# Fox attention on one core: one PSUM bank for the projections, two for the turned probabilities

## What is computed

```
q = rms_norm(q.reshape(B, S, FOX_HEADS, FOX_DH), q_norm_g)
k = rms_norm(k.reshape(B, S, FOX_HEADS, FOX_DH), k_norm_g)
...
logits = jnp.einsum('bhts,bshd...') + cb[..., None] - c_t[:, :, None, :]
probs = jax.nn.softmax(logits, axis=-1)
return jnp.einsum('bhts,bshd->bthd', probs, vf)
...
o = o * jax.nn.silu(z)
```

## Time and profile before

| | us |
|---|---|
| median of 3 runs (lowest, highest) | 2000.39 (1998.85, 2004.83) |
| the profiled execution | 1997.79 |
| its span, first to last instruction | 1995.9 |
| PE busy | 1876.2 (94% of the span) |
| PEld, DVE, ACT, POOL busy | 1453.8, 938.5, 773.4, 238.8 |

### The profile page before, as it was taken

One profiled execution on the slowest core, in us unless ns is written; L12 is line 12 of the kernel. 1 busy time (PEld: TensorE's weight loads), 2 busy tenths in 40 slices (PEclk: granted clock), 3 DMA queues, 4 the chain that ended last, 5 costly groups with the idle time before them and its releaser, 6 DMA issues. The chain is left out here.

```text
span 1995.9 us, 27109 instructions
## 1 busy us (share of the span) xinstructions
PE 1876.2 (94%) x10220; PEld 1453.8 (73%) x10220; DVE 938.5 (47%) x1723; ACT 773.4 (39%) x1271; POOL 238.8 (12%) x182
## 2 busy tenths in 40 slices
PE   7999999999999998898989999999999999889898
PEld 5888888879797876776878787655555555468687
DVE  3757565665757562755341210243434434466533
ACT  3526253534436261414222221454454544441321
POOL 1212021211212010020000000110111101002000
PEclk9999999999999999998999999999999999989899
DMA  5211010201011100403112110201111110041211
GB/s 129 51 36 32 22 33 22 36 19 43 14 41 33 32 1 1 159 32 127 40 47 85 43 44 14 58 27 41 30 37 38 28 29 20 23 138 53 92 53 45
DMA packets 113793, 92.22 MB, mean 46 GB/s; under 512 B 19776, under 2 KB 95744, under 8 KB 113664
## 3 DMA queue, kind: packets, MB, share of 16 engines
q1 hardware_dynamic: 113664, 90.49, 16.0%
HBM read 81.99 MB, written 8.49 MB: 45 GB/s over the span
## 5 line engine op out<-in xcount | busy, mean ns | idle before, releaser
L404 PE MATMUL gdn_unit<-part_hi,gdn_w_hi 128*128 128x512 f32 x512 | 234.0, 457 | 0.0
L406 PE MATMUL gdn_unit<-part_hi,gdn_w_lo 128*128 128x512 f32 x512 | 202.1, 395 | 0.0
L405 PE MATMUL gdn_unit<-part_lo,gdn_w_hi 128*128 128x512 f32 x512 | 200.7, 392 | 0.0
L1906 DVE CUSTOM_DVE_ANT_0 fa_probs<-fa_scores,fa_decay 128x896 f32<-128x896 f32 (+7 forms) x128 | 97.0, 758 | 126.0 <-PE fa_scores L1721 80.6
L1740 PEld LDWEIGHTS fa_turned<-ident,fa_probs 128*128 128x128 f32 x576 | 61.0, 140 | 105.0 <-issue 52.5
L1740 PE MATMUL fa_turned<-ident,fa_probs 128*128 128x128 f32 x576 | 102.9, 288 | 33.3 <-ACT fa_probs_t L1855 16.0
L1855 ACT ACTIVATE fa_probs_t<-fa_turned 128x512 f32<-128x512 f32 (+1 forms) x96 | 52.2, 544 | 182.3 <-PE fa_turned L1740 181.4
L753 DVE SCALAR_TENSOR_TENSOR x<-gdn_raw,gdn_taps,x 128x512 f32<-128x512 f32 x144 | 119.8, 832 | 5.1
L371 POOL TENSOR_TENSOR gdn_w_lo<-ring,gdn_w_hi 128x1024 fp32r<-128x1024 f32 x31 | 75.1, 2421 | 354.9 <-ACT gdn_w_hi L570 354.9
L1673 PE MATMUL fa_unit<-part_hi,fa_w_hi 128*128 128x512 f32 x256 | 115.0, 449 | 1.5 <-DVE fa_w_lo L1933 1.5
L406 PEld LDWEIGHTS gdn_unit<-part_hi,gdn_w_lo 128*128 128x128 f32 x512 | 96.2, 188 | 21.5
(11 more groups left out here) (279 smaller groups left out, 3986.7 us busy)
## 6 DMA issues: line engine op xcount, KB each, us to landing
ring<-in_gdn_w_in_dram SPq DMA_DIRECT2D x32, 512.0 KB, 4.2
ring<-in_ple_w_gate_dram SPq DMA_DIRECT2D x32, 256.0 KB, 3.0
ring<-in_fox_w_in_dram SPq DMA_DIRECT2D x32, 256.0 KB, 3.3
ring<-in_fox_w_in_dram SPq DMA_DIRECT2D x16, 512.0 KB, 4.8
fa_decay<-c_rows_scratch SPq DMA_DIRECT2D x64, 128.0 KB, 3.0
in_x_tile<-in_x_dram SPq DMA_DIRECT2D x8, 512.0 KB, 6.0
gdn_g_bc<-g_rows_scratch SPq DMA_DIRECT2D x8, 512.0 KB, 8.9
m_old<-in_x_dram SPq DMA_DIRECT2D x8, 512.0 KB, 3.5
```

The costliest lines, as they stand in the source:

```text
L404: pe.matmul(out, w_hi[:, j % 2, k, :], xh[:, k, ts], start=(k == 0), stop=False)
L405: pe.matmul(out, w_hi[:, j % 2, k, :], xl[:, k, ts], start=False, stop=False)
L406: mm = pe.matmul(out, w_lo[:, j % 2, k, :], xh[:, k, ts], start=False, stop=(k == KT - 1))
```

## The change

`unit` becomes one bank in place of two, and `turned` becomes two banks, one for the pieces that ScalarE copies and one for those that VectorE copies. A unit's first matmul now waits until the unit just before it was taken, not the one before that. A turn now waits for the last copy of its own engine, so there is a whole piece in between. `spread` uses the first of the two banks. The number of banks is the same, and so is every engine's order of instructions; the waits and the addresses alone differ.

```diff
-        unit = [ps(f"unit{n}", [P, HALF]) for n in range(2)]
+        unit = ps("unit", [P, HALF])
...
-        turned, result = ps("turned", [P, HALF]), ps("result", [P, HALF])
+        turned, result = [ps(f"turned{n}", [P, HALF]) for n in range(2)], ps("result", [P, HALF])
...
                 if k == 0:
                     pe.wait_ge(w_low, j + 1)
-                    if n >= 2:
-                        pe.wait_ge(unit_taken, n - 1)
-                out, ts = unit[n % 2][:], slice(half * HALF, (half + 1) * HALF)
+                    if n:
+                        pe.wait_ge(unit_taken, n)
+                out, ts = unit[:], slice(half * HALF, (half + 1) * HALF)
...
-                if by:
-                    pe.wait_ge(flip_a, before + 1)
-                elif before:
-                    pe.wait_ge(flip_d, before)
+                if before:
+                    pe.wait_ge((flip_a, flip_d)[by], before)
                 if e in (0, 5) and side == by == 0 and 2 * p + e // 5:
...
                     pe.wait_ge(spread_used, 2 * p + e // 5)
                 for b, j in enumerate(keys(e, quarter)):
-                    mm = pe.transpose(turned[:, b * P:(b + 1) * P], probs[:, n % 3, j * P:(j + 1) * P], c["ident"][:])
+                    mm = pe.transpose(turned[by][:, b * P:(b + 1) * P], probs[:, n % 3, j * P:(j + 1) * P], c["ident"][:])
...
             def spread(p, part):
                 pe.wait_ge(shared, 2 * p + part + 1)
 
-                pe.wait_ge(flip_d, sides_before(p, (5, NT)[part]))
+                pe.wait_ge(flip_a, sides_before(p, (5, NT)[part]))
```

More of the change, by code:

```diff
@@ L1598, in turned_to @@
             return (probs_t[:, head, ks[0]:ks[-1] + 1, at:at + P],
-                    turned[:, 0:len(ks) * P].rearrange("p (j t) -> p j t", t=P))
+                    turned[by][:, 0:len(ks) * P].rearrange("p (j t) -> p j t", t=P))
         @block.sync
@@ L1693, in keep_warm @@
                 for n in range(rounds):
-                    pe.matmul(unit[n % 2][:], w_hi[:, 0, 0, :], xh[:, 0, 0:HALF], start=True, stop=True)
+                    pe.matmul(unit[:], w_hi[:, 0, 0, :], xh[:, 0, 0:HALF], start=True, stop=True)
             def sum_squares(p, kind):
@@ L1759, in spread @@
                 pe.wait_ge(shared, 2 * p + part + 1)
-                pe.wait_ge(flip_d, sides_before(p, (5, NT)[part]))
+                pe.wait_ge(flip_a, sides_before(p, (5, NT)[part]))
                 for e in range(4):
                     at = row(e) % 4 * P
-                    mm = pe.transpose(turned[:, at:at + P], wide[:, e * P:(e + 1) * P], c["ident"][:])
+                    mm = pe.transpose(turned[0][:, at:at + P], wide[:, e * P:(e + 1) * P], c["ident"][:])
                 mm.then_inc(spread_out, 1)
@@ L1821, in take_unit @@
                 act.wait_ge(unit_made, n + 1)
-                step(act.activation(qk[:, it % 2, u // 2, u % 2 * HALF:(u % 2 + 1) * HALF], unit[n % 2][:], ACT.Copy),
+                step(act.activation(qk[:, it % 2, u // 2, u % 2 * HALF:(u % 2 + 1) * HALF], unit[:], ACT.Copy),
                      unit_taken)
@@ L1927, in gate @@
                 dve.wait_ge(spread_out, 2 * p + part + 1)
-                step(dve.tensor_tensor(z, turned[:], z, ALU.mult), spread_used)
+                step(dve.tensor_tensor(z, turned[0][:], z, ALU.mult), spread_used)
                 dve.wait_ge(weighed, 4 * p + 2 * part + 2)
```

## The result

The changed kernel takes 1968.26 us in the median of 4 runs (1967.68 to 1970.58), the kernel before 2000.3 (1998.85 to 2004.83): 32.0 us less, ratio 0.9838 with a 95% interval of 0.9821 to 0.9856.

A forecast was written before the change was run, and what follows sets the result against it. The prediction took TensorE's own waits in the attention stage as the bound. Passes 9.2, pass turns 9.0, pass 0 -3.3 and last pass 6.4 made 21.3 us less, forecast 1979.1 us, range 1972 to 1990.

The forecast's parts named there:

- What bounds the kernel: Attention stage: TensorE sets the pace; its idle time, partly hidden in busy time, is what can be won.
- the waits are not to blame: Rival, turns within a pass: the 0.49 us idle is the sequencer's and stays; 2003.7 us, no measurable change; chance 0.09.
- part of the delay stays: Rival: turns behind projections begin 0.87 us after them, not 0.78; gain 12.4 us, time 1988.0; chance 0.14.
- What the turned banks give: Turns within a pass: they no longer wait for the copy just begun; 2.75 us gained a pass.
- What the single unit bank costs: Projections wait for ScalarE's unit copy: 1.43 us lost a pass at steps 16 and 24, 3.3 in pass 0.
- The pass turn: Block 7's turns between passes: sums of q begin 1.32 us sooner in six, 1.1 in the seventh; 9.0 us together.
- the sum: Whole kernel: 9.2 + 9.0 - 3.3 + 6.4 = 21.3 us less than before.
- The last pass: Final pass, without units: its turns wait less, 6.4 us gained, bounds 3 and 7.5.
- The clock rival: Rival: new idle time ahead of units, 17 places, drops TensorE's clock; 2003.4 us, or 2012 with pass turns; chance 0.07.

The follow-up runs named there:

- the repeat: The changed kernel measured again with no edit and more rounds: 1967.86 us, ratio 0.9847 to the kernel before.
- all three: Changed kernel without unit waits, first-half spread in an idle scores bank, ScalarE taking a pass's last unit behind the square of q: 1946.07 us, ratio 0.9738.
- the banks swapped: Against "all three", unit 3 and spread's first-half shares exchange banks, so only the sums of k wait for the unit: 1940.66 us, ratio 0.9711.

## Why the prediction was wrong

**What bounds the kernel** was right: TensorE's own waits, hidden in part in its busy time. The two rivals in which the waits are not to blame, or part of the delay stays, are out: behind a projection step, turns begin 0.77 to 0.79 us after its start in all seven passes of the changed kernel.

**What the turned banks give** is the step that failed, by its size. The forecast took 2.75 us a pass, from step to turn, and kept the length of the turn: "four tiles take 0.42". By the starts the steps give 3.2 (two places that I had left out give 0.23 of it, a few hundredths each the rest), and the turns a further 0.53 (twelve of them, 0.03 to 0.06 each), which the forecast had at nothing. With the wait gone the weights load under the step's last matmul, and four tiles take 0.35. The row for it was in hand: in the earlier trace rows the weight load begins with the step's last matmul. I read from it when the turn would begin, not that it would be shorter.

**What the single unit bank costs** was right in kind and place, 24 waits, and a little low: 1.6 us a pass by the starts against 1.43, 4.0 in pass 0 against 3.3. TensorE's projections begin 0.14 us after the end of ScalarE's copy, 24 times of 24, not the 0.06 that the earlier trace rows had. That row is of dummy matmuls, and ahead of those it is 0.05 in the changed kernel too. The 0.14 stood in the earlier trace rows, where the copy ends at 1387.11 and the turn begins at 1387.25. Why the two differ is not shown.

**The pass turn** gave 1.14 by the starts against 1.32: 0.09 of the forecast's gain is counted with the steps here (block 6's second turn), and the sums begin 0.14 us behind the square, not 0.06. What it was worth besides, the sum did not have. One pass turn of the kernel before was at half clock; I named it as a bound, counted nothing, and in the profiled execution it is 1.6 us. The experiments show more of it: with the unit's wait and the old pass turn together, four or five of seven pass turns are at half clock, and taking the pass turn's wait away gives 17 to 18 us instead of 9.

**The last pass** gave 8.6 against 6.4, above its bound of 7.5. By the starts the places that the forecast counted give 6.3. Three that it left out give 0.9, shorter turns 0.6, and 1.0 is again the clock: in the kernel before it is at half from 1757.5, with the stage's last matmuls still to come, and in the changed kernel it falls only behind them. Small terms take 0.2 back.

So of 29.1 us, 7.8 more than the sum: passes 4.6, clock 1.6, last pass 2.2, pass 0 less 0.7. By cause, over all passes, the largest are about 4.3 us for shorter turns, 2.6 for the clock and 2.5 for the places left out; against them the unit bank cost some 2 us more. All but pass 0 lie on one side, and the low end of the range, 26 us of gain worked out and 2 for scatter, had no room for several small terms that were left out for lack of a row. The medians differ by 32.0 and, in the repeat, 30.9; the 29.1 lies within both intervals.

**The clock rival** had the wrong cause. The waits for the unit alone do not halve the clock: the changed kernel has 24 of them, 0.5 to 0.9 us each, and PEclk is 1.00 in every pass. The Trainium skill (TensorE: Matmul & The Clock Gate, A second HAM failure mode: psum-queue depth-cycling) tells of a kernel in which brief idle times between groups of matmuls made the clock go up and down; for idle times of this size the changed kernel's trace does not agree with it. The half clock came with the long idle time at the pass turn, and more often where a wait for the unit stood just ahead of it.

## What to carry to other kernels

When a wait in front of a matmul goes, count two things: the time until the matmul may begin, and the matmul's own length once its weights load ahead. Buffers help where the wait stands: a second bank was worth nothing without the changed wait, and the bank taken away cost 16 us that idle banks of the same stage gave back. And look at what an engine does between a producer and the copy that frees its buffer: moving one copy ahead of one square gave 9 us without any other bank.

## What the runs showed of the hardware

A group of four transposes took 0.41 us to the next instruction's start when its first weight load had waited, and 0.35 when that load lay under the matmul before it; one transpose 0.10 and 0.03. TensorE's projections began 0.14 us after the end of the ScalarE copy that they waited for, dummy matmuls 0.05.

In the attention stage, up to its last pass turn, TensorE's clock fell to its lower level (1.2 of 2.4 GHz) only at pass turns where TensorE idled for 1.4 us or more at a time, and not at each of those. In the profiled execution of each kernel it was one pass turn of seven in the kernel before (1.5 to 1.7 us idle), and five, five and four of seven in the three kernels where 1.4 to 1.5 us of idle time came behind a wait of 0.4 to 0.6 for the unit. In "all three" it was one, behind the 2.4 us; with the banks swapped the same 2.4 us left the clock whole. At the 61 pass turns of these traces at which it idled for at most 0.9 us at a time, the clock never fell. What decides which of the long ones is hit stays open.
